# Two transformer blocks on one core: modulation panels summed by VectorE in quarters, and the 24 late ones multiplied by GpSimd during a feed forward

## What is computed

```python
def layer(...):                       # first block, for l in 0, 1
    mod   = c_silu    @ ada_w + ada_b     # 1024 -> 3*1024: shift, scale, gate of the latent tokens
    mod_c = cctx_silu @ ada_w + ada_b     # the same weights for the context tokens
    hx = rmsnorm(x, norm_w) * (1 + scale) + shift
    ...three attention mixers, gate_c used only if there is a next layer...
    x = x + gate * (ux @ w_out)

def second_block(...):
    c_act = silu(c)
    for l in range(DEPTH):
        mod = c_act @ ada_w[l] + ada_b[l]         # 1024 -> 6*1024
        sh1, sc1, g1, sh2, sc2, g2 = split(mod, 6)
        h = rmsnorm_2(x, norm_mix_g[l]) * (1.0 + sc1) + sh1
        ...forgetting attention, pooling, retention, convolution...
        x = x + g1 * (mix @ w_out[l])
        h = rmsnorm_2(x, norm_ffn_g[l]) * (1.0 + sc2) + sh2
        f = (silu(h @ ffn_w1[l]) * (h @ ffn_w3[l])) @ ffn_w2[l]     # hidden width 2816
        x = x + g2 * f
    return rmsnorm_2(x, final_g)
```

## Time and profile before

| what | value |
|---|---|
| median of three runs | 2388.33 us |
| the profiled execution | 2388.78 us, its span 2386.7 us |
| granted clock of TensorE over the span | 0.998 of full speed |
| busy: PE, PEld | 2334.7 us (98%), 1933.5 us (81%) |
| busy: DVE, ACT, POOL | 57%, 43%, 20% |

### The profile page before, as it was taken

The page is one execution under the profiler, slowest core; times in us unless marked ns, Lnnn a source line. Parts: engine busy times, 40 slices in busy tenths (PEclk is TensorE's granted clock), DMA queues, the critical chain, the costliest instruction groups (busy, mean ns, idle before and its releaser), DMA issues.

```text
span 2386.7 us, 40461 instructions
## 1 busy us (share of the span) xinstructions
PE 2334.7 (98%) x16214; PEld 1933.5 (81%) x16214; DVE 1358.2 (57%) x2721; ACT 1016.0 (43%) x1808; POOL 466.2 (20%) x289
## 2 busy tenths in 40 slices
PE   8999999999999999999999999999999999999998
PEld 7878878788887888878887678888888768888887
DVE  5777675685238755768558644333337855433333
ACT  5672275732337625672554434222235544222221
POOL 2102212012342032203663320000014232000001
PEclk9999999999999999999999999999999999999999
DMA  7303413044133053406342122233232112323222
GB/s 306 137 2 133 168 53 144 2 160 150 60 126 142 2 217 115 150 3 252 114 145 72 62 80 89 81 105 104 81 108 89 63 56 78 106 83 112 97 78 72
DMA packets 64203, 250.55 MB, mean 105 GB/s; under 512 B 7408, under 2 KB 9968, under 8 KB 54544
## 3 DMA queue, kind: packets, MB, share of 16 engines
q1 hardware_dynamic: 61216, 236.10, 28.4%
q0 software_dynamic: 2592, 11.54, 1.5%
q10 hardware_dynamic: 208, 0.33, 0.0%
HBM read 243.67 MB, written 4.19 MB: 104 GB/s over the span
## 4 chain that ended last, share of the span: by engine, by line
PE 87%; ACT 5%; DVE 3%; issue 2%; DVEq 1%; DMA 1%; POOL 1%; ACTq 0%; SPq 0%
PE ps L2833 40%; PE ps L2648 21%; PE ps L2810 6%; PE ps L723 3%; PE ps L614 3%; ACT probs L929 3%; PE ps L664 3%; PE ps L2850 2%; PE ps L708 1%; PE ps L2627 1%; PE ps L2531 1%; DMA stage_low<-in_ada 1%; DVEq L812 1%; DVE ps L829 1%; PE ps L2675 1%
## 5 line engine op out<-in xcount | busy, mean ns | idle before, releaser
L2648 PE MATMUL ps<-h_split_first,split_panels_first 128*128 128x512 f32 (+1 forms) x2772 | 535.4, 350 | 0.9 <-POOL h_split_first L1253 0.9
L2833 PE MATMUL ps<-h_split,split_panels 128*128 128x512 f32 x2088 | 500.0, 394 | 1.2 <-ACT projected L1722 0.8
L2648 PEld LDWEIGHTS ps<-h_split_first,split_panels_first 128*128 128x128 f32 x2772 | 439.1, 188 | 73.1 <-issue 3.9
L2833 PEld LDWEIGHTS ps<-h_split,split_panels 128*128 128x128 f32 x2088 | 387.8, 188 | 92.9 <-issue 14.7
L1214 POOL TENSOR_TENSOR split_panels_first<-panels_first,split_panels_first 128x1024 fp32r<-128x1024 f32 (+2 forms) x100 | 222.1, 2221 | 664.4 <-ACT split_panels_first L1412 664.4
L1979 DVE SCALAR_TENSOR_TENSOR ps<-modulation_panels,silu_c,ps 128x256 f32<-128x256 f32 x480 | 225.3, 488 | 30.0 <-issue 1.7
L2165 DVE TENSOR_TENSOR split_panels<-panels,split_panels 128x1024 fp32r<-128x1024 f32 (+2 forms) x110 | 126.9, 1158 | 133.7 <-ACT split_panels L1437 133.7
L1232 POOL TENSOR_TENSOR probs_turned<-probs_turned,probs 128x512 f32<-128x512 f32 x30 | 40.7, 1358 | 764.4 <-ACT probs L1665 761.8
L1854 ACT ACTIVATE probs<-ps 128x512 f32<-128x512 f32 x44 | 26.3, 598 | 349.9 <-PE ps L2833 349.7
L1437 ACT ACTIVATE split_panels<-panels 128x1024 fp32r<-128x1024 f32 (+2 forms) x149 | 144.7, 978 | 67.6 <-PE ps L2833 67.1
L614 PE MATMUL ps<-qkv 64*128 64x256 f32 (+1 forms) x1232 | 143.9, 360 | 4.5 <-ACT qkv L1499 2.8
(11 more groups left out here) (330 smaller groups left out, 3712.4 us busy)
## 6 DMA issues: line engine op xcount, KB each, us to landing
modulation_panels<-in_ada SPq DMA_DIRECT2D x64, 1024.0 KB, 4.8
panels<-in_w SPq DMA_DIRECT2D x88, 512.0 KB, 3.2
panels_first<-in_in SPq DMA_DIRECT2D x72, 512.0 KB, 5.7
panels<-in_in SPq DMA_DIRECT2D x42, 512.0 KB, 3.3
panels_first<-in_out SPq DMA_DIRECT2D x32, 384.0 KB, 3.1
panels<-in_w SPq DMA_DIRECT2D x32, 384.0 KB, 3.1
panels<-in_w SPq DMA_DIRECT2D x32, 320.0 KB, 2.9
panels<-in_out SPq DMA_DIRECT2D x16, 512.0 KB, 3.2
```

The source lines that it names most:

```text
L2648: ins = mm(at0, split1[:, s, w, c, :], hs1[:, h, c, lo:e], start=c == 0 and i == 0, stop=c == KC - 1 and i == 2)
L2833: ins = mm(out, panel_of(n, l)[:, a, c - base, :], moving(b, c), start=first and i == 0 and j == 0, stop=last and i == len(chunks) - 1 and ...
```

## The change

- **Schedule.** `spare` now holds 40 panels: all 16 ADA1 and the 24 ADA2 of the second block's layer 0. They stand in phases A, B, C and G of layer 0 (5, 11, 4, 9) and in B of layer 1 (11). The 24 ADA2 panels of the second block's layer 1 become `late_panels`. The last four ADA1 panels are made for one vector only.
- **Sum over partitions.** `sum_mod` goes. In `mod_parts`, behind the eight chunks, DVE transposes the products in 32x32 blocks (`V.transpose`) and sums the free axis by 32 (`tensor_reduce`) into `quarter_sums`; both stand in `add_rows`. Once for a phase, PE runs `sum_mods`: four matmuls with a 128x32 stationary tile `quarters`, and ACT copies all results of the phase in `take_mods`.
- **Late panels.** They are loaded one at a time into `late_panel` (1 MB, one buffer), by SP, in the feed forward of the second block's layer 0. Load i stands in SP's list behind a fixed raw load (`late_issue`) and waits until POOL has finished panel i - 1. POOL runs `late_parts`: 8 `tensor_scalar` and 7 `tensor_tensor` of 128x256 with 15 drains for a panel. DVE runs `late_rows` (transpose and sum) for panel 12 f + b - 1 at the end of feed forward step b, and for the last two of a half in w2; PE sums all 24 in w2 step c = 3 of the second half, ACT takes them there, and `modulations2(1)` follows on DVE in step 5.
- POOL sets two more buffers again in layer 1 of the second block (`ppad`, `augk`).

```diff
-        second = [(ADA2, l, i) for l in range(DEPTH) for i in range(N_ADA2)]
...
+        latents = iter([(ADA1, l, i) for l in range(DEPTH) for i in range(N_ADA1)][N_SS1:])
+        others = iter([(ADA2, 0, i) for i in range(N_ADA2)])
+        spare = {}
+        for l, m, kinds in ((0, "A", "22222"), (0, "B", "11211211212"), (0, "C", "2222"), (0, "G", "121212121"), (1, "B", "11112222222")):
+            for j, kind in enumerate(kinds):
+                spare[l, PHASES[m][0] + j] = next(latents if kind == "1" else others)
+        late_panels = [*others, *((ADA2, 1, i) for i in range(N_ADA2))]
...
+        def late_step(j):
+
+            f, b = j // (HALF + 1), j % (HALF + 1)
+            return FFN_AT + FFN_PER * f + 2 * b + RAW + SPLIT + 2
+        LATE_SUMS_AT = 3
+        late_made = [partial[:, 0, PAN * i:PAN * i + PAN] for i in range(2)]
+        late_adding, late_product = rstd[:, 0:PAN], rstd[:, PAN:2 * PAN]
+        late_issue = {FFN_AT + RAW + SPLIT - 1: 0, **{late_step(j): j + 1 for j in range(len(late_panels) - 1)}}
...
                     sp.dma_start(raw[:, n % RAW, 0:panel_size(n)], src).then_inc(raw_in[n % RAW], 16)
+                    if l == 0 and n in late_issue:
+                        i = late_issue[n]
+                        if i == 0:
+                            sp.wait_ge(out_ready, DEPTH * KC + KC)
+                        else:
+                            sp.wait_ge(part_ready, len(ada_seq) - N_SS1 + i)
+                        _, of, j2 = late_panels[i]
+                        sp.dma_start(late_panel[:, :], dram[ADA2][of, j2]).then_inc(late_in, 16)
...
+            def late_parts(j):
+
+                pool.wait_ge(late_in, 16 * (j + 1))
+                w = late_panel.rearrange("p (c n) -> p c n", c=KC)
+                for c in range(KC):
+                    pool.drain()
+                    if c == KC - 1 and j >= 2:
+                        pool.wait_ge(quarters_ready, len(ada_seq) - N_SS1 + j - 1)
+                    nc.gpsimd.tensor_scalar(late_product if c else late_adding, w[:, c, :], silu_c2[:, c:c + 1], None, ALU.mult)
+                    if c:
+                        pool.drain()
+                        ins = nc.gpsimd.tensor_tensor(late_adding if c < KC - 1 else late_made[j % 2], late_adding, late_product, ALU.add)
+                ins.then_inc(part_ready, 1)
...
                 split_odd(norm_no(l, True))
+                for j in range(len(late_panels) if l == 0 else 0):
+                    late_parts(j)
...
+            def late_rows(j):
+
+                dve.drain()
+                dve.wait_ge(part_ready, len(ada_seq) - N_SS1 + j + 1)
+                add_rows(late_panels[j], late_made[j % 2], partial[:, 1, 0:PAN])
+
+            def add_rows(p, made, turned_by_32):
+
+                k, nv = ada_no[p], vectors_of(p)
+                V.transpose(turned_by_32, made)
+                dve.drain()
+                if p in opens_phase and k > N_SS1:
+
+                    dve.wait_ge(mod_ready, k)
+                V.tensor_reduce(quarter_sums[:, quarter_slot[p]:quarter_slot[p] + nv, :],
+                                turned_by_32.rearrange("p (v j n) -> p v j n", v=nv, n=32), AX_X, ALU.add).then_inc(quarters_ready, 1)
...
                         V.tensor_tensor(acts[:, 1, b, :], t, acts[:, 0, b, :].bitcast(F32), ALU.subtract).then_inc(f_ready, 1)
                         rest(n + 2 * b + 1 + SPLIT, l)
+                        if l == 0 and (f, b) > (0, 0):
+                            late_rows((HALF + 1) * f + b - 1)
                     for c in range(KC):
+                        if l == 0 and c == 1:
+                            late_rows((HALF + 1) * f + HALF - 1)
+                        if l == 0 and (f, c) == (1, 2):
+                            late_rows(2 * (HALF + 1) - 1)
+                        if l == 0 and (f, c) == (1, LATE_SUMS_AT + 2):
+                            modulations2(1)
...
-            def sum_mod(p):
...
+            def sum_mods(panels, at0, slots_used):
+
+                pe.wait_ge(quarters_ready, ada_no[panels[-1]] - N_SS1 + 1)
+
+                pe.wait_ge(mod_taken, ada_no[panels[0]])
+                to = at0[:, 0:2 * slots_used].rearrange("p (s h) -> p s h", h=2)
+                for q in range(4):
+                    ins = mm(to[32 * q:32 * q + 32], quarters, quarter_sums[:, 0:slots_used, q:8:4], start=True, stop=True, skip_group_check=True)
+                ins.then_inc(mod_ready, len(panels))
```

## The result

The changed kernel takes 2559.6 us in the median of 4 runs (2559.2 to 2561.4), the kernel before 2388.5 us beside it (2388.2 to 2389.9): a ratio of 1.072 (95% interval 1.070 to 1.074). It is 171 us slower, where 81 were forecast, and lies 15 us above the top of the range. The profiled execution has a span of 2557.3 us, 170.6 more than before. The place and the kind of the loss are as forecast; its size is not.

What follows compares the result with a forecast made beforehand. PE's own work was taken to bound the kernel, with POOL's late panels pacing layer 0's feed forward after the change. 2388.8 - 32 (sums) - 1 (DVE) + 114 (stall) = 2470 us, range 2415 to 2545.

Steps and rivals of the forecast that it cites:

- What bounds the kernel, and the direction: Nearly everywhere PE's own work sets the time, a matmul removed is worth its full length; the change was forecast slower, 0.92.
- Parts 1 to 3: Sums leaving PE and sum_mods coming: -32 us together; DVE in the first block: -1 us.
- The smaller reading, 31: PE's removed sums in the first block, read at 0.80 us from small matmul to next product: about 31 us; 38 taken.
- DVE in the first block: Transpose and sum added to DVE's panels in the first block: -1 us in all (-3 to +3).
- Part 4, the period: Late panels in layer 0's feed forward: load plus POOL's work and DVE's share, P = 16.8 us per panel (14.6 to about 20.8).
- How long PE stands: PE's stall in layer 0's feed forward, both halves: 21 P - 239, 114 us at P = 16.8 (68 to 198).
- 10 P - 117.4: First half: PE's lateness at the deadline of panel 27's rest in w2; 50.6 us at P = 16.8.
- Panels 11 and 12 fit into w2: End of the first half: these late panels cause no further stall, so the second half starts level.
- 11 P - 121.7: Second half: PE's lateness at its sums in w2 step 3; 63.1 us at P = 16.8.
- The loop that hides: Rival: with P under 11.4 us no wait reaches PE in the feed forward, 2356 us; chance 0.07, including P to 12.9.
- POOL is slower still: Rival: tensor_scalar dearer than an addition, or POOL loses turns to DVE; P of 20 or more, 2537 us and above; chance 0.10.
- The third: Rival: TensorE's clock falls in the gaps; staying at 1.2 GHz, 21.8 us a step, near 2595 us; chance 0.03.

Runs made afterwards that it cites:

- the experiment with all panels early: Changed kernel without late panels: all 64 panels made by VectorE in the first block, with quarter sums; 2383.6 us, ratio 0.997 to the kernel before.
- the kernels with four, six and eight chunks: Changed kernel with POOL taking 4 or 6 of each late panel's 8 chunks: 2389.1 and 2469.0 us; eight is the changed kernel itself, 2559.6 us.
- The short first panel: Changed kernel with POOL taking 2 of 8 chunks of the first late panel alone, the other 23 whole; 2553.0 us.
- two chunks of eight: Changed kernel with POOL taking only 2 of 8 chunks of each late panel, loads, waits and order kept; 2360.1 us, ratio 0.988 to the kernel before.

## Why the prediction was wrong in size

The profiled execution is 170.6 us longer; the prediction had 114 - 33 = 81. By its own steps:

**What bounds the kernel, and the direction: right.** PE's own work set the time, a matmul taken away was worth its length, and the new waits sit where they were placed: from the fifth step of the first half and the sixth of the second on, released by DVE, none in the first block. One does not: w2 of the first half was to have no gap after step 2, and it has one of 2.5 us.

**Parts 1 to 3: 33 forecast, 27 measured.** The feed forward's products that began at 1463.99 begin at 1436.84. A block without a sum is dearer than I took it. The chain of the changed kernel:

```profile
186.00 96.31 PE ps L2736 x546
...
354.71 46.49 PE ps L2736 x264
```

96.31 / 546 x 48 is 8.47 us, 46.49 / 264 x 48 is 8.45. I had taken 8.31 from a run of 90 records, so the sums cost 9.22 - 8.45 = 0.77 and 8.77 - 8.45 = 0.32 us, not 0.91 and 0.46. `sum_mods` costs less than I had: 0.39 us for eight records where it stands after a wait, not 0.97. By landmarks layer 0 gives 16.5 us (its output products begin at 582.62, before at 599.14), of which I had 17 to 18, and layer 1 another 11.5 (behind the same wait for POOL in its output products, 1127.39 against 1155.45), where 32 sums of 0.51 should have given 16.3: not every sum there cost its length. I read 0.51 in stage G alone and took it for stages A and C as well; which sums were hidden is not shown. The smaller reading, 31, which stood in the text, was the nearer one. DVE in the first block cost nothing, as forecast, and the experiment with all panels early shows how near that was to its edge.

**Part 4, the period: 16.8 forecast, 19.75 measured, and this is the first step that failed.** The load took 4.9 us and 5.0 to 5.2 with its semaphores (5.1 taken). An addition took 0.91 from start to start (0.885 taken). In the even panels DVE took nothing from POOL (0.4 taken); it made panels 0 and 1 longer by 4.2 and 1.5 us, and panels 11 to 13, where the halves meet, by 1.0 to 2.9. The product took 1.07 (0.64 taken): 8 x 0.43 = 3.4 us of P, and with the prediction's slope of 21, 72 us of time. The bound was the fault: "They read one tile and write one, so they lie between the memset of this size, 0.311, and the two-tile operation, 0.745" orders instructions by their number of tiles, and no row of the trace did so for POOL with arithmetic. The kernel with the multiplication of two tiles shows that the order is the reverse. The prediction had named a `tensor_scalar` outside 0.31 to 0.75 us as a sign of being wrong, and 0.92 is one. The price of an instruction that the trace does not hold should have been left open upward, and with the sensitivity of 21 us for each microsecond in the same text, 0.2 us on eight products is 34 us.

The sentence on the Trainium skill's page, GPSIMD Engine Reference, section Engine selection, that GpSimd is roughly at line rate for one input, gave an estimate of 0.3 us; the trace has 0.92, and 0.85 with a constant. The measurement decides. The page's other statement, that GpSimd is the wrong choice for plain elementwise work, the runs bear out: 2559.6 us with GpSimd at the products, 2368.2 with VectorE.

**How long PE stands: 21 P - 239 gives 176 us at P = 19.75; measured 197.7 (170.6 + 27.1).** This is the second step that failed: 21 periods were counted, and over the kernels with four, six and eight chunks each microsecond of P costs 23.6 us, from the same zero near P = 11.4. The formula is short by 3 us at four chunks (24 for 27.7), by 12 at six (95 for 107.6) and by 22 at eight. Most of it lies in the first half, and there it can be named in part. The second half begins at 1687.31 where 1616.31 - 27.1 would be without a stall: 98.1 us, where 10 P - 117.4 gives 80.1. First, I let panel 1 begin at 1456.1 - 27.1 + 5.1 = 1434.1; POOL reached panel 0 only at 1419.8, behind its splits, and DVE slowed that panel, so panel 1 began at 1443.89, 9.8 us later. It goes with POOL's time: with six and four chunks panel 1 began at 1435.52 and 1433.10. The short first panel gave 6.6 us back. Second, I ended the stall at the deadline of panel 27's rest. The timeline of PE from there:

```profile
1639.84 9.88 PE L2920 MATMUL ps<-ffn_hidden_split,split_panels 128*128 128x512 f32 x33 [10.21 <-DVE split_panels L2248]
...
1660.44 4.24 PE L2920 MATMUL ps<-ffn_hidden_split,split_panels 128*128 128x512 f32 x18
1667.20 5.29 PE L2920 MATMUL ps<-ffn_hidden_split,split_panels 128*128 128x512 f32 x15 [2.52 <-DVE split_panels L2248]
...
1687.31 5.60 PE L2920 MATMUL ps<-h_split,split_panels 128*128 128x512 f32 x24
```

33 products take 9.88 us for 7.64, then a gap of 2.5 us comes and 15 products take 5.29 for 3.56. From 1639.84 to 1687.31 it is 47.5 us, from 1575.5 to 1616.31 it was 40.8: 6.7 us. The prediction had "Panels 11 and 12 fit into w2", which they did not at 19.8 us: the raw panels behind the load of panel 11 were held in SP (ACT waits here for a load of a raw panel):

```profile
1665.55 0.74 ACT L1502 ACTIVATE split_panels<-panels 128x640 fp32r<-128x640 f32 x1 [18.98 <-DMA panels<-in_w]
```

9.8 and 6.7 of the 18.0 (98.1 - 80.1) are named. The second half stood for 98.5 us (1927.95 to the sums, from 1687.31, against 142.1), where 11 P - 121.7 gives 95.6.

The sum of the misses: 6 in the gain, 62 for 2.95 us of P at 21 each, 22 in the formula: 90 us. P itself lies in the forecast's own 14.6 to 20, but by luck: load, additions and the dearest products allowed come to 5.5 + 6.2 + 7.1 = 18.8, and only the 2 us kept for DVE, which the even panels did not use, reached further. At 19.75 the formula gives 2388.8 - 33 + 176 = 2532, inside the range; the 22 us of the formula and the 6 of the gain carry the time out of it. I had cut the range at 2545 since all terms would have to be at their worst together, but the bounds held only the terms that I had written down; the count of 21 periods, read as if no step came late before the first deadline or after the last, had no bound of its own.

**The rivals.** The loop that hides is what two chunks of eight gave: 2360, at 2356 forecast. "POOL is slower still", by a `tensor_scalar` dearer than an addition, was what happened: its 2537 at P = 20 had the mechanism and lacked the 22 us beyond the formula. It had 0.10, as much as a bound allowed that excluded its condition. The third, a TensorE held at its lower level: behind each gap the granted clock falls (0.60 and 0.72 of full speed in 1500 to 1505 and 1505 to 1510, around and behind the gap that ends at 1502.06, 1.00 in the next 5 us; 0.84 over both halves), but the steps stay at POOL's pace of 19.75, not at 21.8; the slack hides it, save where a half ends.

## What to carry to other kernels

Before work moves to an idle engine, count the ring that its buffer closes (load, compute, the consumer, the queue that issues the next load) and compare that with the step; the engine's share of busy time says nothing of it. An instruction that the trace does not hold has no upper bound in another instruction's price; where a loop multiplies it by eight and a slope by more than 20, measure it alone first. And look whether an engine with room does the step in one instruction: VectorE's fused multiply and add took 0.48 us where GpSimd took 1.65, and 101 busy microseconds of 133 cost PE nothing.

## What the runs showed of the hardware that I had not expected

- GpSimd multiplies a tile of 128x256 by a column in 0.92 us, by a constant in 0.85, and by a second tile (a broadcast column) in 0.61; adding two tiles takes 0.73.
- A drain between two GpSimd instructions costs 0.15 us ahead of an instruction of two tiles and 0.16 to 0.17 ahead of one with a scalar.
- GpSimd and VectorE collide: products of 0.93 us became 1.62 and 2.23, VectorE's operation of 0.69 became 1.07. In the changed kernel the wait for the load kept them apart, and the kernel that hid the load lost 2 of its 5 us to it.
- A gap of 2.5 to 10 us of PE is followed by 15 to 48 products that take up to two thirds as long again (15 in 5.29 us behind a gap of 2.5, 15 in 5.99 behind one of 9.95, for 3.56).
